# Norm statistics as four rows of 128 columns: one summed tile of squares, a 4x128 root and reciprocal, and a spread back through TensorE; `small` widened by 192 bytes

## The reference, cut to what matters

```python
def rms_norm(t, w):
    tf = t.astype(jnp.float32)
    y = tf * lax.rsqrt(jnp.mean(tf * tf, axis=-1, keepdims=True) + NORM_EPS)
    return (y * w.astype(jnp.float32)).astype(t.dtype)

def modulate(h, shift, scale):
    return h * (1.0 + scale[:, None, :]) + shift[:, None, :]
...
        h = rmsnorm(x, norm_mix[i])
...
        x = x + conv_ffn(rmsnorm(x, norm_ffn[i]), f_w_up[i], f_conv_w[i], f_conv_b[i], f_w_down[i])
    return rmsnorm(x, norm_final)
```

## Time and profile before

| | before |
|---|---|
| median of three runs | 3805.72 us (3805.24 to 3810.72) |
| profiled execution, its own time | 3805.69 us |
| span of the profile | 3804.0 us |
| PE busy | 3421.7 us, 90% |
| DVE busy | 2033.0 us, 53% |
| ACT busy | 1203.2 us, 32% |
| POOL busy | 111.2 us, 3% |
| mean granted TensorE clock | 0.95 |
| `L807` matmuls on PE | 128.0 us in 256 records |

### The profile page before, as it was taken

How to read it: one execution, slowest core, us unless ns; L and a number is a source line. 1 busy time by engine, 2 the same in 40 slices (tenths; PEclk the granted TensorE clock), 3 DMA queues, 4 the chain that set the end, 5 groups by cost and what they waited for, 6 DMA issues and landing times. The chain is left out here.

```text
span 3804.0 us, 37654 instructions
## 1 busy us (share of the span) xinstructions
PE 3421.7 (90%) x13270; PEld 2500.3 (66%) x13270; DVE 2033.0 (53%) x2739; ACT 1203.2 (32%) x1532; POOL 111.2 (3%) x204
## 2 busy tenths in 40 slices
PE   3998589998779999998999998799978859989997
PEld 1445468886557887666888743688856626767886
DVE  5747455635538863565665388566434343335523
ACT  2211343314433222443453200444333322233221
POOL 0000000000000000000000110000000000000000
PEclk9897799999989999999999999899999979999999
DMA  5332036642114553212233211123322201222332
GB/s 209 113 121 75 28 117 189 194 139 70 45 56 156 197 160 94 67 45 67 88 95 94 77 56 44 56 94 97 95 90 94 83 28 50 88 78 82 98 96 72
DMA packets 100417, 361.00 MB, mean 95 GB/s; under 512 B 11152, under 2 KB 11168, under 8 KB 100064
## 3 DMA queue, kind: packets, MB, share of 16 engines
q1 hardware_dynamic: 77936, 276.07, 22.9%
q0 software_dynamic: 20080, 75.27, 6.2%
q10 hardware_dynamic: 2304, 8.39, 0.6%
HBM read 357.59 MB, written 2.10 MB: 95 GB/s over the span
## 5 line engine op out<-in xcount | busy, mean ns | idle before, releaser
L1756 DVE TENSOR_TENSOR weight_lo<-weight_ring,weight_hi 128x1024 fp32r<-128x1024 f32 (+1 forms) x462 | 556.8, 1207 | 1006.8 <-ACT weight_hi L1211 1002.2
L1211 ACT ACTIVATE weight_hi<-weight_ring 128x1024 fp32r<-128x1024 f32 (+1 forms) x462 | 482.4, 1045 | 1502.4 <-PE proj_banks L743 1140.0
L743 PE MATMUL proj_banks<-h_lo,weight_hi 128*128 128x512 f32 x1776 | 693.5, 391 | 0.0
L743 PE MATMUL proj_banks<-h_hi,weight_hi 128*128 128x512 f32 x1344 | 524.4, 390 | 8.8 <-DVE weight_lo L1756 8.8
L743 PE MATMUL proj_banks<-h_hi,weight_lo 128*128 128x512 f32 x1344 | 524.2, 390 | 0.0
L743 PEld LDWEIGHTS proj_banks<-h_lo,weight_hi 128*128 128x128 f32 x1776 | 334.7, 188 | 69.6
L743 PE MATMUL proj_banks<-mid_lo,weight_hi 128*128 128x512 f32 x768 | 299.5, 390 | 0.0
L743 PEld LDWEIGHTS proj_banks<-h_hi,weight_hi 128*128 128x128 f32 x1344 | 252.8, 188 | 62.6 <-issue 10.4
L743 PEld LDWEIGHTS proj_banks<-h_hi,weight_lo 128*128 128x128 f32 x1344 | 252.6, 188 | 52.4
L1211 ACT ACT_TABLE_LOAD x132 | 169.4, 1283 | 350.0 <-PE proj_banks L743 109.7
L689 PE MATMUL proj_banks<-h_tiles,weight_ring 128*128 128x512 f32 x592 | 265.7, 608 | 13.8 <-ACT h_tiles L1211 7.3
(11 more groups left out here) (321 smaller groups left out, 5070.7 us busy)
## 6 DMA issues: line engine op xcount, KB each, us to landing
weight_ring<-in_w_up SPq DMA_DIRECT2D x176, 512.0 KB, 3.6
ada_ring<-in_ada POOLq DMA_DIRECT2D x96, 512.0 KB, 3.9
weight_ring<-in_w_dn SPq DMA_DIRECT2D x64, 512.0 KB, 3.6
weight_ring<-in_w_br SPq DMA_DIRECT2D x32, 512.0 KB, 3.7
weight_ring<-in_w_upr SPq DMA_DIRECT2D x32, 512.0 KB, 3.5
weight_ring<-in_w_dnr SPq DMA_DIRECT2D x32, 512.0 KB, 3.5
scratch<-in_ada POOLq DMA_DIRECT2D x24, 512.0 KB, 4.4
weight_ring<-in_w_dn SPq DMA_DIRECT2D x32, 384.0 KB, 3.1
```

The costliest lines, as they stand in the source:

```text
L743: last = mm(proj.banks[:, u % RING, :], stationary(split0 + n)[:, w], moving(k), start=k + m == 0, stop=k == kt - 1 and m == 2)
L1211: return nc.scalar.activation(out, in_, func, **kw)
L1756: return v.tensor_tensor(out, a, b, op)
```

## The change

- **Sum of squares.** DVE adds the squares of tiles 0 to 6 into the first of them (`sum_up`, six additions of 128x512). For norms 1 to 8 this stands in `residual`, ahead of the wait for the last tile (k = 7); for norms 0, 9 and 10 it stands in `norm`, behind everything that DVE has to do first.
- **Four rows.** PE multiplies the summed tile and the square of tile 7 by `pick`, a 128x4 stationary matrix that has ones in one column: four products of 128 columns for each, all into one 4x128 area of PSUM (row j has the sums of tokens 128j to 128j+127). These are eight small products in place of eight of 512 columns.
- **Root and reciprocal** are taken of 4x128 instead of 128x512. A Sqrt of one column (`small[:, 160:161]`) is issued by ACT right behind square 6.
- **Spread back.** Four products of a 4x128 stationary `sel` and the 4x128 reciprocal, 128 columns each, put the statistic on all 128 partitions of one more PSUM bank, key `("bc", r)`.
- **Apply.** DVE computes H(k) = X(k) · gain · statistic in one scalar_tensor_tensor that reads the statistic from PSUM. In split modulated norms ACT adds the shift and rounds in one instruction to `h_hi`, and DVE computes `h_lo` = H + shift − `h_hi` in one scalar_tensor_tensor.
- **Weights.** Weight chunk 0 is rounded at k = 6 and chunk 1 behind the root (before: both at k = 6); the rest of chunk 0 is taken ahead of the reciprocal and that of chunk 1 behind it (before: both ahead).
- **Order in `first_pair`.** The products with `h_lo` go k by k, tile 0 and tile 1 in turn.
- **Memory.** The constant `pick` takes 64 bytes per partition more and `small` 192 bytes more, 256 together, so that all buffers behind them lie 256 bytes further.

```diff
+        "pick": np.tile(np.eye(4).reshape(1, 16), (P, 1)),
...
-        self.small = sb("small", [P, 160])
+        self.small = sb("small", [P, 208])
...
-        for t in range(2):
-            for k in range(KD):
-                if t == 0:
-                    pe.wait_ge(s["h_ready"], h_count(r, k))
+        for k in range(KD):
+            pe.wait_ge(s["h_ready"], h_count(r, k))
+            for t in range(2):
                 last = mm(proj.bank((name, t)), c.hi(split0 + t)[:, k * P:(k + 1) * P], lo(k), start=False, stop=k == KD - 1)
-            last.then_inc(proj.full_sem, 1)
+                if k == KD - 1:
+                    last.then_inc(proj.full_sem, 1)
...
     def norm(r):
-        sum_squares(("ss", r), lambda k: (s["sq_ready"], 8 * r + k + 1), lambda k: T(squares_at(r) + k), KD)
+
+        bank = open_bank(mix, ("ss", r))[0:4, 0:P]
+        for half, (sem, n) in enumerate(((s["sq_summed"], 6 * (r + 1)), (s["sq_ready"], 8 * (r + 1)))):
+            pe.wait_ge(sem, n)
+            squares = T(squares_at(r) + (KD - 1 if half else 0))
+            for j in range(NB):
+                last = mm(bank, c.const("pick")[:, 4 * j:4 * j + 4], squares[:, j * P:(j + 1) * P], start=half + j == 0, stop=half + j == NB)
+        last.then_inc(mix.full_sem, 1)
+        bank = open_bank(mix, ("bc", r))
+        pe.wait_ge(s["rstd_ready"], r + 1)
+        for j in range(NB):
+            last = mm(bank[:, j * P:(j + 1) * P], c.const("sel")[0:4, j * P:(j + 1) * P], T(RSTD)[0:4, P:2 * P], start=True, stop=True)
+        last.then_inc(mix.full_sem, 1)
...
             st.done(f(T(squares_at(r) + k), X(k), ACT.Square), s["sq_ready"])
-            if r in SPLIT_UP and k == KD - 2:
-
-                up = SPLIT_UP[r]
-                for n in range(SPLIT_RING):
-                    round_chunk(up, n)
-        root(("ss", r), T(RSTD), D)
+            if k == KD - 2:
+
+                st.link(f(c.small[:, 160:161], eps, ACT.Sqrt))
+                if r in SPLIT_UP:
+                    round_chunk(SPLIT_UP[r], 0)
+        act.wait_ge(*mix.filled(("ss", r)))
+        ins = f(T(RSTD)[0:4, 0:P], mix.bank(("ss", r))[0:4, 0:P], ACT.Sqrt, scale=1.0 / D, bias=eps[0:4, :])
+        ins.then_inc(mix.emptied(("ss", r))[0], 1)
+        if r in SPLIT_UP:
+            round_chunk(SPLIT_UP[r], 1)
...
-                ins = f(H(k), H(k), ACT.Identity, scale=c.g(use, k), bias=c.m(layer, part, k))
-                ins.then_inc(s["h_raw"] if r in SPLIT_NORMS else s["h_ready"], 1)
                 if r in SPLIT_NORMS:
-                    round_h(r, k)
+                    st.done(f(c.norm_hi(r, k), H(k), ACT.Identity, bias=c.m(layer, part, k)), s["h_rounded"])
+                else:
+                    f(H(k), H(k), ACT.Identity, bias=c.m(layer, part, k)).then_inc(s["h_ready"], 1)
...
+    def sum_up(r, k):
+
+        total = T(squares_at(r))
+        dve.wait_ge(s["sq_ready"], 8 * r + k + 1)
+        st.done(tt(total, total, T(squares_at(r) + k), ALU.add), s["sq_summed"])
+
     def norm(r):
+        if r not in NORM_AFTER:
+            for k in range(1, KD - 1):
+                sum_up(r, k)
         if r in SPLIT_UP:
-            for n in range(SPLIT_RING):
-                rest_chunk(SPLIT_UP[r], n)
-        inverse(("ss", r), T(RSTD))
+            rest_chunk(SPLIT_UP[r], 0)
+        dve.wait_ge(*mix.emptied(("ss", r)))
+        st.done(v.reciprocal(T(RSTD)[0:4, P:2 * P], T(RSTD)[0:4, 0:P]), s["rstd_ready"])
+        if r in SPLIT_UP:
+            rest_chunk(SPLIT_UP[r], 1)
+        dve.wait_ge(*mix.filled(("bc", r)))
+        rstd = mix.bank(("bc", r))
         for k in range(KD):
             if r in MODULATED:
-                st.done(tt(H(k), X(k), T(RSTD), ALU.mult), s["xn_ready"])
+                st.done(stt(H(k), X(k), c.g(MODULATED[r][0], k), rstd, ALU.mult, ALU.mult), s["xn_ready"])
...
-                tt(c.norm_lo(r, k), H(k), c.norm_hi(r, k).bitcast(F32), ALU.subtract).then_inc(s["h_ready"], 1)
+                hi = c.norm_hi(r, k).bitcast(F32)
+                if r in MODULATED:
+                    use, layer, part, _ = MODULATED[r]
+                    ins = stt(c.norm_lo(r, k), H(k), c.m(layer, part, k), hi, ALU.add, ALU.subtract)
+                else:
+                    ins = tt(c.norm_lo(r, k), H(k), hi, ALU.subtract)
...
     def residual(stage, gate=None, bias=None, after=None):
+        r = [r for r in NORM_AFTER if NORM_AFTER[r] == stage][0]
         for k in range(KD):
...
+            if k == KD - 1:
+                for done in range(1, KD - 1):
+                    sum_up(r, done)
             dve.wait_ge(*proj.filled(key))
```

More of the change, by code:

```diff
@@ L210, in mixing_keys @@
 def mixing_keys():
-    k = [("ss", 0)]
+    k = [("ss", 0), ("bc", 0)]
     k += [("rot_i", t) for t in range(5)]
@@ L228, in mixing_keys @@
         k += [("av", *units[n - 2])] if n >= 2 else []
-    k += [("ss", 1), ("ss", 2)]
+    k += [("ss", 1), ("bc", 1), ("ss", 2), ("bc", 2)]
     k += [("stat_s", t) for t in range(8)] + [("pool", g) for g in range(4)]
@@ L234, in mixing_keys @@
         k += [("sb", h - 2)] if h >= 2 else []
-    k += [("ss", 3), ("ss", 4)]
+    k += [("ss", 3), ("bc", 3), ("ss", 4), ("bc", 4)]
     k += [("acol", 0)]
@@ L244, in mixing_keys @@
             k += [("stat_m", h - 1)] if h >= 1 else []
-    k += [("ss", 5), ("ss", 6), *(("dw", t) for t in range(KD)), ("lnm", 0), ("lnv", 0), ("ss", 7), ("ss", 8), ("ssc", 0), ("ss", 9)]
+    k += [("ss", 5), ("bc", 5), ("ss", 6), ("bc", 6), *(("dw", t) for t in range(KD)), ("lnm", 0), ("lnv", 0), ("ss", 7), ("bc", 7)]
+    k += [("ss", 8), ("bc", 8), ("ssc", 0), ("ss", 9), ("bc", 9)]
     k += [("rot_r", t) for t in range(8)]
@@ L250, in mixing_keys @@
     k += [("sgu", t) for t in range(2)]
-    k += [("ssy", 0), ("ss", 10), ("ssy", 1)]
+    k += [("ssy", 0), ("ss", 10), ("bc", 10), ("ssy", 1)]
     return k
@@ L519 @@
 PLAIN = {4: ("norm_mix_2", 0), 5: ("norm_ffn_2", 0), 6: ("norm_mix_2", 8), 7: ("norm_ffn_2", 8), 8: ("norm_final_2", 0)}
+PLAIN_SPLIT = (4, 5, 7)
 SQ0, RSTD = 44, 54
@@ L1224, in round_h @@
     def round_h(r, k):
-        n = 8 * SPLIT_NORMS.index(r) + k + 1
-        act.wait_ge(s["h_raw"], n)
+        act.wait_ge(s["h_raw"], 8 * PLAIN_SPLIT.index(r) + k + 1)
         st.done(f(c.norm_hi(r, k), H(k), ACT.Copy), s["h_rounded"])
@@ L1802, in norm @@
                 out = X(k) if r == 8 else H(k)
-                ins = stt(out, X(k), c.v(name, at + k), T(RSTD), ALU.mult, ALU.mult)
+                ins = stt(out, X(k), c.v(name, at + k), rstd, ALU.mult, ALU.mult)
                 if r == 8:
@@ L1806, in norm @@
                 elif r in SPLIT_NORMS:
-                    ins.then_inc(s["h_raw"], 1)
+                    st.done(ins, s["h_raw"])
                 else:
@@ L1810, in norm @@
                     dve.wait_ge(s["h_ready"], h_count(r, k))
+        dve.sem_inc(*mix_release(mix, ("bc", r)))
         if r in SPLIT_NORMS:
@@ L1813, in norm @@
                 dve.wait_ge(s["h_rounded"], 8 * SPLIT_NORMS.index(r) + k + 1)
-                tt(c.norm_lo(r, k), H(k), c.norm_hi(r, k).bitcast(F32), ALU.subtract).then_inc(s["h_ready"], 1)
+                hi = c.norm_hi(r, k).bitcast(F32)
[4 more added lines that the diff above has]
+                    ins = tt(c.norm_lo(r, k), H(k), hi, ALU.subtract)
+                ins.then_inc(s["h_ready"], 1)
                 dve.wait_ge(s["h_ready"], h_count(r, k))
```

2 lines of the change are left out of this document (1 added, 1 removed).

## The result

The change takes 3763.68 us (median of four runs, 3759.94 to 3773.57), the kernel before 3807.0 (3805.24 to 3810.72). The ratio is 0.9889, 95% interval 0.9867 to 0.9911, so 34 to 51 us faster; 43.3 by the medians. The forecast was 53 faster, 3752.5, and the ends of its range were worked out as 3738 and 3776. The profiled execution of the change took 3759.94, 45.8 us less than the one of before.

What follows compares the result with a forecast made beforehand. PE, busy 3421.7 of 3804.0 us, bounds the kernel, so gains come where it waits in the serial norm chain. 54.2 + 7.5 + 7.5 − 5.4 − 3.0 = 60.8, less 9 plus 1.5 for clock: 53.3, giving 3752.5; range 3738 to 3776.

Steps and rivals of the forecast that it cites:

- Additions: Six on DVE ahead of residual 7, norm 1: need 4.33 us, fit in 4.76 us of idle time, cost nothing.
- the rival on it: Table load ahead of the root not hidden by the early Sqrt: back in eight norms, 10 us, 3763; chance 6%.
- Spreading: Four PE products behind the reciprocal, putting the statistic on all partitions: 0.86 us and a hop.
- The pair: First pair after a norm: 48 products, 11.4 us if nothing waits, PE and DVE tie.
- the rival of a DVE that needs 0.92: DVE bounds the pair, its 16 instructions taking 0.92 each: 2.7 us lost in each of six norms, 3769; chance 15%.
- Tail: From output tile 0 finished to PE's resumption at norm 1: 3.86 us with a table load, kept as before.
- The six norms with a pair: Norms 1 to 5 and 7, end of last projection product to PE's resumption: 54.2 us gained together, before 9 for the clock.
- Norms 8 and 9: Earlier context transfer and shorter norm 9 stretch: 7.5 us gained, at least 3.4 and at most 8.6.
- a stage without a norm that changes in length: One of the listed signs that the forecast is wrong: a stage with no norm in it changes in length.
- The clock: Half clock for 3 us of the first pair: 1.5 us at each of six norms, 9 together; 1.5 given back at norm 6.
- the slower rival built on it: Clock never comes back in the pair: all 48 products at half clock take 20.5 us, total 3813; chance 4%.
- The 256 bytes: Added memory ahead of all buffers: costs nothing, since distances between buffers behind stay and no row shows an address effect.

Runs made afterwards that it cites:

- experiment 3: The change with extra useless small products in PE's gaps at the split norms (before the reciprocal wait, first pair and third output tile): 3745.4 us, ratio 0.9844.
- Experiment 1: The change with the `h_lo` products of the first pair run by tiles again, eight of tile 0, then eight of tile 1: 3751.6 us, ratio 0.9859.
- experiment 6: The kernel before with only the memory part of the change, `pick` and wider `small`, 256 bytes, unused: 3805.6 us, ratio 0.9997.
- the last version: The change without additions at norms 0, 9, 10, `h_lo` by tiles, extra products except behind the first pair, early one-column Silu in feed-forward loops: 3722.7 us, ratio 0.9783.

## Why the prediction was right, and where its sum was off

The direction, the place of the gain and the range held; the gain was 43.3 us (interval 34 to 51) against 53. Step by step, by the profiled executions:

- *Additions*: hidden at norms 1 to 8, as said; 4.32 us for six against 4.33, and residual 7 waits 0.40 for PE.
- *Root and reciprocal*: 0.36 and 0.94 against 0.36 and 0.95. The extension of 6.25 ns per column held. The load is hidden; the rival on it falls.
- *Spreading*: mis-sized. I took 0.86; it took 1.12 at norms 2 and 3, and at half clock 2.04 at norms 1 and 5. I had put the small products at full clock and the loss of the clock only in the pair. E to the first pair was 7.0 to 7.9 instead of 6.9.
- *The pair*: PE and DVE tie, as said. DVE's sixteen instructions at 0.78 are the forecast's, so the rival of a DVE that needs 0.92 falls. Half clock cost just what I allowed: against the same pairs with extra products (experiment 3) 0.8 to 2.0 each, 8.7 for six, against 9.
- *Tail*: 3.86 from tile 0 to the resumption held (530.0 to 533.79), but tile 0 was full at E+20.2 and not at E+17.9: the pair started 1.0 later and took 12.5 instead of 11.4. What was missing is the second fall of the clock behind a gap that had grown from 2.05 to 3.64: 1.6 us at norms 1, 5 and 7. Experiment 1 removes it with the gap, experiment 3 with products in the gap.
- *The six norms with a pair* from E to the resumption: 32.1, 30.9, 32.8, 28.7, 29.0 and 28.6 became 24.0, 22.9, 22.3, 22.9, 24.0 and 24.1. That is 41.9 gained; forecast 54.2 less 9, 45.2. With 4.8 lost to the second fall, and 1.6 won by the one that is gone at norm 3, it is 38.7.
- *Norm 0*: 6.3 lost, forecast 5.4. *Norms 8 and 9*: from E of norm 8 to norm 10 the offset between the traces grows by 3.1, forecast 7.5, a little under the lower bound of 3.4. At norm 9 eight small products behind the additions took 3.57 (as at norm 0), and the projection that follows took 15.8 instead of 14.0. *Norm 10*: 0.9 lost, forecast 3. *Norm 6*: 7.0 to its first product, forecast 7.5 and 1.5 for the clock.
- *Elsewhere*: these terms add up to 41.6, and the traces differ by 45.8. The rest lies where the forecast put nothing: 1.9 lost ahead of norm 1, 4.5 gained between the first product after norm 6 and E of norm 7. By my own list, a stage without a norm that changes in length was a sign of being wrong. What changed there isn't shown; such stretches hold products at half clock in both traces, at different places. So part of the closeness of the sum is luck.
- *The clock*: 9 us were allowed, for the pairs alone. Held against the trace of experiment 3, the six norms lose 8.7 in the pairs, 2.3 ahead of them and 4.8 behind them: 15.8 (14.2 less the fall that the kernel before had too). This is the term that was mis-sized: the clock ahead of the pair and behind it was put at nothing. The rule of the Trainium skill, "TensorE: Matmul & The Clock Gate", section "What's actually happening", that the throttled state is the default and activity releases it, is borne out by experiment 3, whose products do nothing but be active; the slower rival built on it did not come, since the clock was back within 3 us in the pair of norm 1, and no pair of the change is longer than 13.6 us, where 20.5 was that rival's.
- *The 256 bytes*: nothing, as said, by experiment 6. But the reason that I gave doesn't hold: distances between buffers behind `small` stay with every shift, with those that cost 51 to 74 us too. What changes is the distance to the buffers ahead. `pick` and one new column of `small` need 64 and some bytes; shifts of 16, 80 and 128 bytes cost 51 to 74 us, more than all of the rest gives (43). Without the padding the change would most likely have been slower than before, as with 80 bytes it is (1.0086). A shift of 64 bytes itself was not tried.

**What stays open.** Why the same gap of 2.05 us costs the clock at norm 1 in one kernel and not in another. The runs of one kernel spread over up to 14 us, and traces drift by 1 to 5 us against each other in stretches without a norm, where the clock changes. Of the 16 to 128 byte shifts it is shown that the split products are further apart and the unsplit ones are not. That the distance of weights and moving tiles decides is made likely by the pair of norm 10, not shown; that reads of the two collide was not measured. Sizes other than 16, 80, 128 and 256 bytes were not tried.

## What to carry to other kernels

When a serial piece between two dense stretches of TensorE is shortened, look at what its engines do in the pieces that are left. Here short gaps with a few small products in them ran at half clock in places (2.04 us instead of 1.12) and handed it on to the dense work behind (1.4 us a pair, 1.6 behind a gap of 3.64). Products without use in a gap gave it back, so long as they ended before the real work was due; where they didn't, they held PE 0.9 us. In float32 a small product with a 4-column stationary cost as much time for each column that moves as a full one (7.15 us for 32 products of 128 columns, 7.03 for 8 of 512); adding tiles on an idle VectorE first is what saved. An addition belongs where that engine idles: at the three norms where it had no idle time, leaving it to TensorE was 20 us better. And after any new buffer or wider constant, count the matmul records of a busy window before anything else is compared: 430 instead of 443 was worth more than the whole change.

## What the hardware showed that I had not expected

A shift of 16, 80 or 128 bytes between weights and moving tiles made split products start 0.233 us apart instead of 0.227, over the whole kernel (430 to 432 records in 100 us instead of 443), at full granted clock; the unsplit products kept their 0.429, and ACT's and DVE's busy times stayed within 0.3 us. A shift of 256 bytes did not. The clock of TensorE fell behind each of 18 idle gaps of 3.6 us, behind 15 of 47 between 1.9 and 2.7 us and behind none of 22 under 1 us; one such fall cost 1.6 us. Two table loads stand in every iteration of the feed-forward loops (552.08 and 554.45 in the change, for one); with an instruction of the function in question at the head of the loop one is left (99 loads in the last version, 132 in the change), and it is off the path.
